# Five of the last six weight fills moved as a transfer of 112 rows and two transfers of eight rows

## The reference, cut to what matters

```python
def expert_block(args):
    tok, e = args
    xb = xt[tok]
    gu = xb @ w_gate_up[e] + b_gate_up[e]      # 1024 x 2048 per expert, float32
    g, u = gu[:, :D_FF], gu[:, D_FF:]
    g = jnp.minimum(g, SWIGLU_LIMIT)
    u = jnp.clip(u, -SWIGLU_LIMIT, SWIGLU_LIMIT)
    hmid = (u + 1.0) * (g * jax.nn.sigmoid(SWIGLU_ALPHA * g))
    return hmid @ w_down[e] + b_down[e]        # 1024 x 1024 per expert, float32
```

## Time and profile before

| what | us |
|---|---|
| median of 3 runs | 1173.81 (1172.93 to 1174.21) |
| the profiled execution's own time | 1173.83 |
| span in its profile, first to last instruction | 1171.8 |
| TensorE busy | 1107.1 |
| moved, MB | 445.31 |

### The profile page before, as it was taken

One profiled execution on the slowest core, in us unless ns is written; L12 is line 12 of the kernel. 1 busy time (PEld: TensorE's weight loads), 2 busy tenths in 40 slices (PEclk: granted clock), 3 DMA queues, 4 the chain that ended last, 5 costly groups with the idle time before them and its releaser, 6 DMA issues.

```text
span 1171.8 us, 12951 instructions
## 1 busy us (share of the span) xinstructions
PE 1107.1 (94%) x5458; PEld 500.3 (43%) x5459; DVE 331.7 (28%) x790; ACT 235.6 (20%) x473; POOL 31.3 (3%) x46
## 2 busy tenths in 40 slices
PE   8999999999999999999999999999999899999896
PEld 7887678873333333333333333333333333333332
DVE  5787664651111212111111111111111111111112
ACT  6585754630000101000100000000000000000002
POOL 0010340100000000000000000000000000000000
PEclk9999999999999999999999999999999999999999
DMA  9915338989999999999999999999999999999995
GB/s 359 356 54 181 108 144 320 333 331 407 427 426 428 427 428 428 426 428 428 427 428 427 427 428 428 427 428 427 427 426 429 428 428 428 427 428 428 428 427 209
DMA packets 46027, 445.31 MB, mean 380 GB/s; under 512 B 6192, under 2 KB 10896, under 8 KB 20368
## 3 DMA queue, kind: packets, MB, share of 16 engines
q1 hardware_dynamic: 44224, 444.19, 91.2%
q10 hardware_dynamic: 1744, 0.28, 0.1%
HBM read 442.82 MB, written 1.05 MB: 379 GB/s over the span
## 4 chain that ended last, share of the span: by engine, by line
PE 62%; DMA 33%; ACT 2%; DVE 2%; issue 0%; DVEq 0%; SPq 0%; ACTq 0%
PE ps L2190 21%; DMA R<-in_w_gate_up 16%; PE ps L2201 12%; PE ps L1669 4%; DMA R<-in_w_down 4%; DMA MK<-in_w_gate_up 4%; DMA QK<-in_w_gate_up 4%; PE ps L1689 4%; DMA XMT<-in_w_gate_up 4%; PE ps L2221 4%; PE ps L1691 4%; PE ps L1690 4%; PE ps L2161 3%; PE ps L2182 1%; PE ps L1918 1%; ACT A L1014 1%
## 5 line engine op out<-in xcount | busy, mean ns | idle before, releaser
L2190 PE MATMUL ps<-R,convT 128*64 128x512 f32 x1104 | 246.5, 594 | 17.8 <-DMA R<-in_w_gate_up 17.8
L1567 DVE TENSOR_SCALAR A<-ps 128x512 f32<-128x512 f32 x30 | 20.8, 692 | 642.4 <-PE ps L2190 642.4
L2190 PEld LDWEIGHTS ps<-R,convT 128*64 128x64 f32 x1104 | 76.7, 137 | 174.2 <-issue 136.3
L2201 PE MATMUL ps<-R,A 128*64 128x512 f32 x592 | 131.9, 593 | 2.0 <-DMA R<-in_w_down 2.0
L1009 ACT ACTIVATE A<-A 128x512 f32<-128x512 f32 x30 | 18.9, 630 | 471.8 <-DVE A L1567 471.8
L2201 PEld LDWEIGHTS ps<-R,A 128*64 128x64 f32 x592 | 41.5, 137 | 79.6 <-issue 75.1
L2221 PE MATMUL ps<-A,convT 64*128 64x512 f32 x248 | 61.6, 615 | 2.1 <-ACT A L1016 1.4
L1016 ACT COPY A<-ps 128x512 f32<-128x512 f32 x30 | 17.6, 585 | 221.3 <-PE ps L2201 221.3
L2161 PE MATMUL ps<-H,convT 128*64 128x512 f32 x248 | 58.4, 592 | 0.0
L2190 PE MATMUL ps<-XMT,convT 128*64 128x512 f32 x208 | 47.0, 593 | 2.4 <-DMA XMT<-in_w_gate_up 2.4
L2190 PE MATMUL ps<-MK,convT 128*64 128x512 f32 x192 | 43.4, 594 | 3.4 <-DMA MK<-in_w_gate_up 3.4
(11 more groups left out here) (347 smaller groups left out, 1314.5 us busy)
## 6 DMA issues: line engine op xcount, KB each, us to landing
R<-in_w_gate_up SPq DMA_DIRECT2D x67, 2048.0 KB, 43.5
R<-in_w_down SPq DMA_DIRECT2D x36, 2048.0 KB, 46.9
XMT<-in_w_gate_up SPq DMA_DIRECT2D x12, 2048.0 KB, 46.5
MK<-in_w_gate_up SPq DMA_DIRECT2D x12, 2048.0 KB, 47.7
A<-in_w_gate_up SPq DMA_DIRECT2D x11, 2048.0 KB, 46.9
XM<-in_w_gate_up SPq DMA_DIRECT2D x11, 2048.0 KB, 45.8
QK<-in_w_gate_up SPq DMA_DIRECT2D x10, 2048.0 KB, 42.6
QK<-in_w_down SPq DMA_DIRECT2D x6, 2048.0 KB, 45.9
```

Of the source, the lines that this page charges most:

```text
L1567: V.tensor_scalar(gcl, bank(G_BANK), LIM, None, ALU.min).then_inc(m_gcl, 1)
L2190: last = mm(bank(b)[s * SLOTS:(s + 1) * SLOTS, :], xg[:, 4 * (j % 2) + 2 * c + j // 2, :], w[:, c * 2 * FF + at + s * BANK:c * 2 * FF + at ...
L2201: last = mm(bank(o)[s * SLOTS:(s + 1) * SLOTS, :], h[:, c, i * SLOTS:(i + 1) * SLOTS], w[:, c * D + s * BANK:c * D + (s + 1) * BANK], star ...
```

## The change

Fills n = 186 to 190 (two of the gate and up of B, both of down of A, the first of down of B) no longer go as one transfer of 128 rows. Each goes as one transfer of partitions 0 to 111, one of partitions 112 to 119 and one of partitions 120 to 127, in this order, each with a completion count of 16 on the slot's semaphore. `ring_at` adds the two further completions (32) for these fills. Bytes, sources, destinations, order of the fills and all waits for slots are as before, and the last fill (191) keeps its two halves.

```diff
+        UNEVEN = tuple(range(FILLS * E - 6, FILLS * E - 1))
+        EVEN_ROWS, FEW_ROWS = 112, 8
+
         def ring_at(k, j):
             n = fill_no(k, j)
-            return 16 * (n // RING + 1 + sum(h <= n and (n - h) % RING == 0 for h in HALVED))
+            return 16 * (n // RING + 1 + sum(h <= n and (n - h) % RING == 0 for h in HALVED)
+                         + sum((P - EVEN_ROWS) // FEW_ROWS for h in UNEVEN if h <= n and (n - h) % RING == 0))
...
+                def fill_uneven(e, j, slot):
+
+                    if j < GU_FILLS:
+                        src = w_gate_up[0, e:e + 1, j * 2 * P:(j + 1) * 2 * P, :].rearrange("o (p c) n -> p (o c n)", c=2)
+                    else:
+                        f = (j - GU_FILLS) * 4 * P
+                        src = w_down[0, e:e + 1, f:f + 4 * P, :].rearrange("o (p c) n -> p (o c n)", c=4)
+                    sp.dma_start(ring[slot][0:EVEN_ROWS], src[0:EVEN_ROWS]).then_inc(arrived[slot], 16)
+                    for r in range(EVEN_ROWS, P, FEW_ROWS):
+                        sp.dma_start(ring[slot][r:r + FEW_ROWS], src[r:r + FEW_ROWS]).then_inc(arrived[slot], 16)
...
+                    elif n in UNEVEN:
+                        fill_uneven(k, j, ring_slot(k, j))
                     else:
                         fill(slice(k, k + 1), j, ring_slot(k, j)).then_inc(arrived[ring_slot(k, j)], 16)
```

## The result

The changed kernel takes 1212.88 us (median of four runs, 1210.01 to 1215.84) where the kernel before takes 1174.01 us (four runs beside them, 1172.93 to 1174.21). The ratio is 1.0322, with a 95% interval of 1.0297 to 1.0347. The direction is the one that was forecast. The size isn't: 1183.5 us was forecast, and 1212.88 lies above the range's upper end of 1197.

A forecast was written before the change was run, and what follows sets the result against it. Bound: the fill stream's end. Crowding 14.4 plus 3.1 us for 112 rows makes 17.5; less lead 6 is 11.5, less slack 1.8 is 9.7 us, added to 1173.83: 1183.5 us, range 1174.5 to 1197.

The forecast's parts named there:

- What bounds the kernel: Expert stage: a stream of fills at 428 GB/s, 4.90 us each, where time is won or lost only at its end.
- Rival 1: End of stream: only balance counts, eight-row transfers run at engine speed, TensorE's two waits go, 1171.8 us; chance 0.11.
- rival 2: End of stream: light crowding, engines meet seldom (30% of the way), 1175 to 1178 us; chance 0.16.
- rival 3: End of stream: eight-row transfers fall on the lagging half, 1189.5 us, or 1197 us with full crowding; chance 0.25.
- Issue and waits at 0: SP's queue and TensorE: ten more transfers (3.3 us of issue, hidden) and 32 more wait counts cost 0.
- the 112-row transfer: Cut fills: ten engines for a time share the width eight had, adding 0.61 us per fill, 3.1 us over five.
- The eight-row transfers: Cut fills: 2.5 us each by crowding into few partitions; 14.4 us over five fills on the half carrying them.
- 60% of the way: Eight-row transfers: how often engines meet, between 3.1 us (never) and 22 us (always) over five fills, giving 14.4 us.
- The lead of 6 us: End of stream: half the engines finish near 1151.5, the others near 1157.5; 6 us taken off the charged half's 17.5.
- Nothing at 186: Fill 186 was to land no later; the shift, 3.5 us per fill less 6, starts with +1.0 at 187.
- What would show it: End of stream: DMA share near 1, rate falling to 250 to 350 GB/s, last weights landing near 1170.
- the prediction's own test: Fill landings: the lag is mis-sized if they move by other than 3.5 us per fill.

The follow-up runs named there:

- The control by columns: Kernel before with fills 186 to 190 each as three transfers of all 128 rows, cut by columns (14, 1 and 1 KB): 1173.43 us, ratio 0.9999.
- the run with partitions 0 to 63: Kernel before with fills 186 to 190 each as eight transfers of eight rows four apart, partitions 64 to 127 not loaded: 1172.67 us, ratio 0.9989.

## Why the prediction was right in its direction and wrong in its size

**What bounds the kernel, and the rivals.** Held. The end was decided by the fills' landing, the engines were busy all the while, and the rate was what fell, as the prediction had taken from the transfers into 64 partitions. Rival 1 (1171.8), rival 2 (1175 to 1178) and rival 3 (up to 1197) all fell.

**Issue and waits at 0.** Held. The control by columns has as many transfers, and more completion packets, and stands at 0.9999. Issuing a cut fill took 6.0 to 9.3 us, far more than three times 0.33, but it stayed hidden as forecast.

**The step that failed: the 112-row transfer.** The prediction put it at "0.61 us per fill, 3.1 us over five", for rows that crowd for a time and are done when eight rows would be. By itself it makes a fill take 8.24 us where the term gave 4.3 + 0.61 = 4.9. That is 3.3 us more per fill, 17 us over five, and it starts ahead of the cut fills: TensorE waits 1.96 us for 185, which is whole. Behind this stands what the earlier trace rows show and I read too narrowly: 213 GB/s at a share of 1.02. I took it for the price of a width of 64, to be scaled with the width, so that 112 rows were almost whole. 112, 96 and 64 rows pay alike (222, 235 and 235 GB/s). The reading that fits, and that no row shows directly, is that it is the price of two engines on one place. The split, seven rows each for 16 engines, was right in the number of engines, by the count of completions; that 128 rows or 112 are dealt out in runs of neighbours, so that ten engines share what eight had, no run shows.

**The eight-row transfers.** Over-sized. They were put at 2.5 us each, an estimate by scaling that no run shows, and 60% of the way to it, which left 3.5 us a fill for both (4.9 + 3.5, less 4.9 for the 112 rows). From 112 rows alone to the change a fill goes from 8.24 to 10.85 us, 2.6 us for both, 1.3 us each: about an ordinary row at the slowed rate (1.18 to 1.32 us in the table). The errors of the two terms are opposite, +3.3 and -0.9, and the first is the larger. That the sum wasn't further off is in part luck.

**The lead of 6 us.** This was counted as a credit: the charged half could be 6 us later before it mattered. It was none. The charge isn't on one half (with fill 190 alone cut, 187 GB/s at a share of 1.06, and no packet of 16 KB under 1.09 us). Nor do the engines that carry the eight-row transfers seem to be the leading or the lagging half, as their ends are spread over some 7 us in the run with partitions 0 to 63: neither the forecast's case nor rival 3's is what the kernel did. All engines slow down together, and by my reading the lead only makes the slow stretch start earlier, while the lagging engines are on whole fills. "Nothing at 186" was forecast; TensorE waited 4.19 us already at 185 and 5.47 at 186.

**The sum by measured terms.** The products of fill 185 start at 1142.01 less 5.56, 1136.45, where they started at 1132.05: 4.4 us later. From there to the products of 190 it is 54.2 us where it was 23.7 (1132.05 to 1155.72): 30.6 more. The last slow group adds 1.5. Together that is 36.5 us; the forecast had 9.7. Per fill the landings move by 10.85 - 4.90 = 5.95 us instead of 3.5, and nothing comes off for the lead.

**What would show it.** The share near 1 was right, the rate of 250 to 350 wasn't (178 to 215), nor were the last weights there near 1170 (fill 190, not yet the last, came at 1196.2). Landings moved by 5.95 us a fill, not 3.5, and by the prediction's own test the lag was mis-sized.

**Shown and not shown.** Shown: the width of a transfer isn't the cause (eight rows at 410 GB/s per unit of share, and 0.61 us a row), which rows it takes is (four partitions on, 216 to 261 for 6 us), and uncut fills in flight pay too, on all engines (188 and 189 come 2.6 and 8.6 us later with 190 alone cut, at 187 GB/s and a share of 1.06). Not shown directly: that two engines share a place in the 112-row transfer; no row names the engine and the partition of a packet, and it rests on the likeness of the rate. Nor does the number of engines that meet explain why 112, 96 and 64 rows all come to about half. Open as well are the last 2 us of the slow stretch after a single cut fill, and whether the side that reads has a part in it.

## What to carry to other kernels

In a stream that ran at 428 GB/s in transfers of 128 rows, rows weren't a free unit to cut it by (1.0234 to 1.0322 in two or three pieces, all bytes moved); columns were (0.9999 with 14, 1 and 1 KB of each row). Before moving rows from one engine to another, ask which partitions the others may be writing at that moment: four partitions' difference in the destination cost 6.7 us here. The price was the rate of the whole stream, at about half: 180 to 259 GB/s for 25 us after one cut fill. By the estimate above (6 us of lead and the narrow rows themselves, 20 to 23 us) it would be larger the further the engines are out of step, which no run varied. A busy share of 1 said nothing of the rate: it was 1.02 at 213 GB/s and 1.03 at 410. Read the two side by side, and take a row that shows half rate as a warning about the pattern, not as a point on a curve over the width.

## What the runs showed of the hardware that I had not expected

- One fill cut into 112, 8 and 8 rows among whole ones halved the rate of all sixteen engines, also of those that wrote whole fills: 187 GB/s at a share of 1.06, with only the last whole fill cut, and no packet of 16 KB under 1.09 us from 1143 to 1150 us.
- The rate was nearly the same with pieces of 112, 96 and 64 rows: 222, 235 and 235 GB/s from 1130 to 1140 us.
- Transfers of eight rows that lie four partitions apart, into partitions 0 to 63, ran at full speed on half of the engines: 214 GB/s at a share of 0.51, and 0.61 us for a packet of 16 KB in the median.
- TensorE's granted clock fell while it waited: it was 1.00 from 1149 to 1151 and 0.50 from 1151.6 to 1152.4, ahead of the products of 1152.46, and 0.66 in the whole stage from 1150 us on, where in the kernel before TensorE was busy for 9.31 of the same 10 us at 1.00. Groups of 16 products took up to 6.57 us instead of 3.65. Most of that lay ahead of a further wait for a fill; only the 1.5 us of the last group had none behind it.
